# Giving the recurrence lanes a turn after every six projection matmuls instead of every twenty-four

## The reference, cut to what matters

```python
def rwkv7_recurrence(r, w, k, v, a_vec, b_vec):
    def step(st, inp):
        r_t, w_t, k_t, v_t, a_t, b_t = inp
        sa = jnp.einsum('bhvk,bhk->bhv', st, a_t)
        st = st * w_t[:, :, None, :] + sa[..., None] * b_t[:, :, None, :] + v_t[..., None] * k_t[:, :, None, :]
        return st, jnp.einsum('bhvk,bhk->bhv', st, r_t)
```

## Time and profile before

| what | us |
|---|---|
| median of three runs | 3615.29 |
| the profiled execution's own time | 3611.87 |
| its span, first to last instruction | 3610.1 |
| the recurrence: first lora matmul to last closing product | 1213.9 to 1481.3, that is 267.4 |

### The profile page before, as it was taken

One profiled execution on the slowest core, in us unless ns is written; L12 is line 12 of the kernel. 1 busy time (PEld: TensorE's weight loads), 2 busy tenths in 40 slices (PEclk: granted clock), 3 DMA queues, 4 the chain that ended last, 5 costly groups with the idle time before them and its releaser, 6 DMA issues.

```text
span 3610.1 us, 68879 instructions
## 1 busy us (share of the span) xinstructions
PE 3431.5 (95%) x30172; PEld 3366.1 (93%) x30172; DVE 2272.2 (63%) x3695; ACT 1605.1 (44%) x2259; POOL 79.7 (2%) x101
## 2 busy tenths in 40 slices
PE   7899999999999998899999999988998999999997
PEld 7899999999998886799999999987998999999997
DVE  5656556546676687587666655587555876666555
ACT  4444445444445522255444444462333554444443
POOL 0000000000000011000000000002000000000000
PEclk9999999999999998799999999999999999999998
DMA  6455555555463321165656656642443555555664
GB/s 223 144 178 170 169 175 176 179 179 173 147 194 130 102 80 48 49 196 171 194 192 195 198 187 195 192 135 77 155 154 100 183 175 194 197 194 190 196 194 134
DMA packets 162638, 587.88 MB, mean 163 GB/s; under 512 B 18145, under 2 KB 18145, under 8 KB 161953
## 3 DMA queue, kind: packets, MB, share of 16 engines
q1 hardware_dynamic: 160848, 575.06, 48.8%
q0 software_dynamic: 1488, 8.42, 0.7%
HBM read 581.31 MB, written 2.10 MB: 162 GB/s over the span
## 4 chain that ended last, share of the span: by engine, by line
PE 52%; DVE 6%; ACT 1%; issue 0%; POOL 0%; ACTq 0%; DVEq 0%; POOLq 0%
PE bank L1926 16%; PE bank L1927 16%; PE bank L1928 16%; DVE pairs L2655 1%; DVE xs L2771 1%; DVE xs L2769 0%; PE bank L1940 0%; PE bank L1941 0%; PE bank L1942 0%; PE bank L2102 0%; DVE xr L2659 0%; PE bank L2089 0%; DVE right L3096 0%; PE bank L2079 0%; ACT pairs L2350 0%
## 5 line engine op out<-in xcount | busy, mean ns | idle before, releaser
L1926 PE MATMUL bank<-xr,pairs 128*128 128x256 f32 (+1 forms) x5664 | 1603.5, 283 | 60.7 <-DVE pairs L2655 49.7
L1927 PE MATMUL bank<-xr,pairs 128*128 128x256 f32 (+1 forms) x5664 | 1581.1, 279 | 0.0
L1928 PE MATMUL bank<-xr,pairs 128*128 128x256 f32 (+1 forms) x5664 | 1580.8, 279 | 0.0
L2350 ACT ACTIVATE pairs<-raw 128x1024 fp32r<-128x1024 f32 x1108 | 1144.4, 1043 | 976.4 <-PE bank L1928 863.1
L2655 DVE TENSOR_TENSOR pairs<-raw,pairs 128x1024 fp32r<-128x1024 f32 x1108 | 1310.9, 1202 | 330.9 <-ACT pairs L2350 328.3
L1926 PEld LDWEIGHTS bank<-xr,pairs 128*128 128x128 f32 x5664 | 1077.7, 190 | 72.2 <-DVE pairs L2655 57.2
L1927 PEld LDWEIGHTS bank<-xr,pairs 128*128 128x128 f32 x5664 | 1076.2, 190 | 1.8
L1928 PEld LDWEIGHTS bank<-xr,pairs 128*128 128x128 f32 x5664 | 1075.9, 190 | 0.0
L1926 PE MATMUL bank<-parts,pairs 128*128 128x256 f32 x1792 | 499.3, 279 | 3.2 <-DVE parts L2659 3.0
L1927 PE MATMUL bank<-parts,pairs 128*128 128x256 f32 x1792 | 497.5, 278 | 0.0
L1928 PE MATMUL bank<-parts,pairs 128*128 128x256 f32 x1792 | 497.4, 278 | 0.0
(11 more groups left out here) (589 smaller groups left out, 3340.7 us busy)
## 6 DMA issues: line engine op xcount, KB each, us to landing
raw<-in_w_in SPq DMA_DIRECT2D x176, 512.0 KB, 4.3
raw<-in_gate SPq DMA_DIRECT2D x176, 512.0 KB, 4.8
raw<-in_val SPq DMA_DIRECT2D x176, 512.0 KB, 4.1
raw<-in_down SPq DMA_DIRECT2D x160, 512.0 KB, 4.5
raw<-in_l_w_in SPq DMA_DIRECT2D x146, 512.0 KB, 3.6
raw<-in_w_out SPq DMA_DIRECT2D x64, 512.0 KB, 4.6
raw<-in_l_w_out SPq DMA_DIRECT2D x64, 512.0 KB, 4.3
raw<-in_v_in SPq DMA_DIRECT2D x48, 512.0 KB, 4.9
```

The costliest lines, as they stand in the source:

```text
L1926: mm(o, wh[:, q, :], rh[:, k, :], start=begin and q == 0, stop=False)
L1927: mm(o, wh[:, q, :], rl[:, k, :], start=False, stop=False)
L1928: last = mm(o, wl[:, q, :], rh[:, k, :], start=False, stop=end and q == c - 1)
L2350: e.activation(pair_of(n)[0], v3(raw_of(n), widths[n] // slices[n]), ACT.Copy).then_inc(*hi_made(n))
```

## The change

`col_tile` gets a parameter `step`: after so many of a half's 8 row blocks the plan gives the lanes a turn. Its default 8 is the half tile of before; the two calls in `rwkv` pass 2, so six matmuls. The semaphore that tells that the weights of a half have been read is still raised once per half.

```diff
-    def col_tile(o, keys, rhs, ready, bk):
+    def col_tile(o, keys, rhs, ready, bk, step=8):
+
         k = 0
         for key in keys:
             n = load(*key)
             c = widths[n] // 128
-            do("col", n, o, rhs, k, key is keys[0], key is keys[-1], [ready_at(ready, k + q) for q in range(c)], bk.after)
+            when = [ready_at(ready, k + q) for q in range(c)]
+            for q in range(0, c, step):
+                do("col", n, o, rhs, k, key is keys[0], key is keys[-1], when, bk.after, range(q, min(q + step, c)))
+                pump()
             k += c
-            pump()
         return (used, n)
...
-            col_tile(p2[:, 0, :], W(17 + c), X2, last.at, j.rv)
-            j.m = col_tile(p2[:, 1, :], W(25 + c), X2, last.at, j.rv)
+            col_tile(p2[:, 0, :], W(17 + c), X2, last.at, j.rv, 2)
+            j.m = col_tile(p2[:, 1, :], W(25 + c), X2, last.at, j.rv, 2)
...
-        def col(n, o, rhs, k0, begin, end, ready, after):
+        def col(n, o, rhs, k0, begin, end, ready, after, part=None):
...
-            for q in range(c):
+            for q in part or range(c):
...
-            last.then_inc(*used(n))
+            if q == c - 1:
+                last.then_inc(*used(n))
```

## The result

The changed kernel takes 3662.22 us (median; 3644.37 to 3680.31) against 3616.24 for the kernel before in the same batch: ratio 1.0107, 95% interval 1.0066 to 1.0149. It is slower, by more than 0.5%. The forecast was 3625 us with a range to 3650; the time lies above it. The profiled execution took 3644.37 us, its span is 3642.6, 32.5 more than before.

What follows compares the result with a forecast made beforehand. TensorE was taken to bound the kernel; five stream stretches 15.7 us longer and the last 6 shorter made 9.7 more, 3621.6 us profiled, with 3.4 for the median 3625 us; range 3594 to 3650.

Steps and rivals of the forecast that it cites:

- That TensorE bounds it and only the recurrence is in play: Whole kernel: TensorE busy for 95% of the span, so only the recurrence's 267 us can change.
- Streamed matmuls, breaks and lane products: Stream stretches: streamed matmuls stay 98.0 us, 86 breaks take 16.3 (12.9 more), lane products 82.8 instead of 85.0.
- Idle, 21 us: Stream stretches: bonus products stall 18.7 us waiting for openings, first lane's inverse 2.2 more; bounds 2 and 32.
- cover the wait for one VectorE step of 0.4 to 0.9 us: Idle in bare stretches: two turns, now spanning twelve streamed matmuls (1.4 us) and other lanes' steps, remove these waits.
- Clock, 5 us: Stream stretches: 5 us allowed for matmuls at half clock after waits.
- Last stretch, 6 us less: After the last streamed matmul: 60.0 us becomes 54; bounds 12 less and 5 more.
- From the profile to the median, 3.4 us: Whole kernel: the median was put 3.4 us above the profiled execution, as in the kernel before.
- The cover works: Rival for the stream stretches: openings always ready, idle 2, clock 0, 199.1 us; time 3597 us; chance 0.22.
- Each opening stalls in full, and the clock falls: Rival for the stream stretches: seven stalls of 4.5 us, idle 32, clock 11.2, 240.3 us; time 3648; chance 0.30.
- the splits (L1929 for L2659) becoming the largest wait: Sign against the forecast, in TensorE's waits: VectorE's queue, not the opening's length, would be the limit.

Runs made afterwards that it cites:

- slow_open: The changed kernel with four empty turns added to each lane's opening, nine turns between projection and bonus product: 3651.79 us, ratio 1.0078.
- light_keys: The changed kernel with three of the seven VectorE operations that make the keys left out: 3635.09 us, ratio 1.0038.
- gate_open: The changed kernel, but lanes still in their opening are passed over in the fine turns: 3652.71 us, run once more 3630.87 us.
- before_c: The kernel before, unchanged, in a third profile: a single execution of 3618.13 us.
- r_only: The kernel before with turns every six matmuls in the first tile (r) of a pair alone: 3652.50 us, ratio 1.0093.
- v_only: The kernel before with turns every six matmuls in the second tile (v) of a pair alone: 3629.69 us, ratio 1.0027.
- after_again: The changed kernel itself, measured again: 3647.97 us, ratio 1.0089.
- before_fill: The kernel before with dummy products at waits of the last two lanes' inverses and the last bonus product: 3620.06 us, ratio 1.0004.
- light_before: The kernel before with the same three VectorE key operations left out of the opening: 3619.04 us, ratio 0.9985.

## Why the prediction was wrong, step by step

- **That TensorE bounds it and only the recurrence is in play:** right. Everything else lay within 4 us.
- **Streamed matmuls, breaks and lane products:** right. At full clock a run of six streamed matmuls takes 0.78 to 0.91 us until the next lane step, 0.68 plus 0.10 to 0.23; the rows had priced a break at 0.10 to 0.22, and the 0.10 on the return from a full-array product stands too. In the sum, breaks and lane products were to grow from 88.4 to 99.1 us, by 10.7. What is left of 249.1 us when the 98.0 of the streamed matmuls, 31.0 of idle and 21.0 for the clock (below) are taken off is 99.1; the same for the kernel before gives 207.4 - 98.0 - 16.2 - 5.0 = 88.2, so 10.9 more. (My 153 and 149 lane rows counted repeated rows once. The absolute numbers are therefore too small, and 0.556 us for one too large; the difference of four, on which the term rests, is right.)
- **Idle, 21 us:** too small, 31 measured, and wrongly made up. The bonus product was given 18.7 and waited 12.3. Of the other 18.7 I had 2.2; the rest I had struck out with the sentence that two turns "cover the wait for one VectorE step of 0.4 to 0.9 us". That sentence is the step that failed. I took a lane's answer to be the next thing on VectorE; it stands behind whatever the other lanes recorded, and an opening is 22 operations up to L2982, with splits between them. The later levels of the inverses alone waited 12.1 us. The rows at 1256.70 show it in the changed kernel; slow_open shows that covering the bonus product alone moves the wait to the inverses, light_keys that a shorter end of the opening leaves it (12.4 us), and gate_open that keeping the opening out of the fine turns takes it down to 1.5 us and removes a third of the idle time.
- **Clock, 5 us:** the largest miss in the stretch. The nine falls last 47.8 us, TensorE is busy in 42.1 of them, and at half the clock half of that is lost: 21.0 us (5.0 before, by the same count, and up to 11.8 in before_c). I took the one fall in the old profile as a rare case and "left" 5. The later waits take the clock down again and again. Idle and clock go together only in part: r_only has 36.0 and 0.90, v_only 23.9 and 0.96, but slow_open 31.9 and 0.95. By the Trainium skill, page "TensorE: Matmul & The Clock Gate", section "The HAM clock gate", the throttled clock is the default and activity releases it. I had cited it for the rival and then given it too little weight; the traces side with it, nine falls against three.
- **Last stretch, 6 us less:** right, 5.7; the three profiles of either kernel have 59.2 to 60.0 before and 54.3 to 54.4 after. Its parts were not measured apart.
- **From the profile to the median, 3.4 us:** too small. The profiled execution was to take 3621.6 us and took 3644.37, 22.8 more; the median of the four executions lies another 17.9 above it, where 3.4 was added. These 14.5 us are spread between executions, in part luck of the four: the seven of after_again have a median of 3647.97, only 4.0 above their profiled one. By that median the change costs 32 us and the time lies just inside the range, but the sum behind 3625 is wrong all the same.
- **The rivals:** "The cover works" fell with the first L2138 wait. "Each opening stalls in full, and the clock falls" is what happened: idle 31.0 for its 32, though less than half of it at the bonus product, where the rival had all of it. Its clock term of 11.2 was still too low by 9.8, and so its stretch of 240.3 us by 8.8.
- **What I said would prove me wrong:** the splits (L1929 for L2659) becoming the largest wait, as the sign that VectorE's queue is the limit. TensorE doesn't wait for the splits at all in the changed kernel, and the queue is the limit nonetheless: it shows at L2095, L2106 and L2117. I looked for the right cause at the wrong line.

What stays open: how the clock's 21 us divide between the two groups of waits, why slow_open keeps a clock of 0.95 with as much idle as the changed kernel, and why the kernel before has a clock of 0.94 in one profile and 0.98 in another with idle the same.

## What to carry to other kernels

Give side work its turns in units at least as long as the answer it waits for takes through the other engine's whole queue, not as long as that one answer; here turns after twenty-four matmuls gave the shortest stage of those tried, twelve and six were too few. When several chains share an in-order engine, look at the longest burst that any of them puts into it, because all the others wait behind it. And a wait of some 2 us on TensorE can cost more than its length: look for slower matmuls behind each such wait and add them up.

## What the runs showed that I had not expected

**A second pace with nothing idle.** In four of the seventeen profiles a stretch of some 450 to 700 us of streamed matmuls runs 4% slower, with TensorE busy all the time and its granted clock at 1.00. Windows of the same program (the one with gated openings) at the same place, 300 us behind the stage, in its first and in its second profile:

```profile
1807.50:2007.50 200.00, 200.00 (x1701) 200.00 (x1700) 122.72 (x161) 89.69 (x107) 0.00 (x0) 1.00 0.56 185
```

```profile
1811.70:2011.70 200.00, 200.00 (x1767) 200.00 (x1766) 127.42 (x167) 93.41 (x111) 0.00 (x0) 1.00 0.58 196
```

That is 0.1176 against 0.1132 us for a matmul. The slower pace was there too in the profiles of before_fill and light_before at the same place, and in that of light_keys some 1400 us behind the stage; the three profiles each of the kernels before and after don't show it. The part behind the stage takes 2129.6 to 2137.9 us in the four, and 2111 to 2117 in all others. That is some 15 to 25 us, against the 32.5 that the change itself moves, and would explain why gate_open measured 3652.71 and 3630.87 us with nearly the same stage. I don't know its cause; the traces show neither a wait nor a lower clock.

**Full-speed work right behind a short wait.** The wait of 1.57 us at 1257.17 left the clock up (L2106 took its usual 0.68 us; the next fall, at 1260.41, lies within the next wait, of 2.68 us), the one of 4.55 took it down until about 5 us behind its end. Among waits of 1.6 to 2.3 us both happened: 1.69 us was followed by a fall in the changed kernel, 2.26 us by none in the kernel before.
